# The recurrence's chunk matrices at 64 columns, all heads in one pass, products on 64x64 tiles of TensorE

## Chip, cores and metric

One core of one Trainium2 chip. The metric is the device time of one execution in microseconds (us), as the median of several runs; lower is better.

## What is computed

A network of three layers on 256 tokens of width 1024, all in f32. The first layer has latent attention beside a recurrence of the RWKV-7 kind and a mixture of 32 experts; two more layers with other mixers and dense feed-forward parts follow. The change lies in the recurrence of the first layer, 8 heads of 64 by 64:

```python
def step(state, inp):
    r_t, w_t, k_t, v_t, kk_t, a_t = inp
    sa = jnp.einsum('bhij,bhj->bhi', state, -kk_t)
    state = (state * w_t[:, :, None, :]
             + sa[..., :, None] * (kk_t * a_t)[..., None, :]
             + v_t[..., :, None] * k_t[..., None, :])
    return state, jnp.einsum('bhij,bhj->bhi', state, r_t)
```

Both kernels compute it in chunks of 64 tokens (CH), 4 chunks (NCH). In a chunk the steps become products of matrices, with a triangular 64 by 64 matrix for each head and chunk that has to be inverted.

## The kernel before

The program is a row of stages. In each, every engine has its own list of instructions, written out by hand, and the engines wait for each other by semaphores; at the end of a stage all engines meet at a barrier. Stages follow each other on TensorE (PE), VectorE (DVE), ScalarE (ACT), GpSimd (POOL) and SyncE (SP), which issues the loads. The recurrence stands at lines 955 to 1212 and runs twice, `for half in range(2)`, for four heads each time. All its operands are in SBUF already. Behind it, a stage (from line 1215) normalizes its output and loads w_o; later stages load the experts' weights.

One pass treats 8 systems (head of an even or odd column half `h2`, pair of heads `hp`, block of 128 tokens `a`). A system is a 128 by 128 matrix with two chunks on the diagonal; the blocks off the diagonal are zeroed by masks. Its six parts:

- start: products of beta and of kappa with alpha and rho (L1003; contraction over 64 rows, 128 weight columns, 256 moving columns), the transposed product (L1012); DVE multiplies each with a mask (L1161, L1162, L1168) and forms a first inverse of blocks of two (L1173 to L1176), in `inv` and transposed in `inv_t`;
- five levels, for blocks of 2, 4, 8, 16 and 32: GpSimd masks `low` for the level (L989), PE makes x = low_b times inv_t (L1023), ACT copies it to SBUF (L1125), PE multiplies with the inverse from both sides (L1032, L1036) and DVE adds the result to `inv_t` and `inv` (L1182, L1183). Each is done for two groups q of four systems, four matrices of 128 columns to a bank of 512. The last level has only the `inv_t` side;
- products with the inverse: a2v (L1042), za (L1050, L1052), ta (L1057), then the matrices that carry a chunk's state on, m (L1066) and n (L1075, L1076), these already as 64 by 64 products;
- the scan over four chunks, with the state of each (L1083, L1196 to L1203, ACT's copy L1144);
- u (L1093), added to za (L1207), and the output (L1102, L1110, L1111), copied to `hT` (L1147).

An f32 `matmul` of the code is two MATMUL records and two LDWEIGHTS records in the trace. Which rows of SBUF the operands lie in and which partitions of PSUM the result goes to sets the tile of the array that is used: "64*64" in a row of the trace is a tile of 64 rows and 64 columns, "128*128" the whole array. Four 64*64 tiles fit in it.

## Time and profile before

| | us |
|---|---|
| median of 3 runs | 2520.09 (2504.41 to 2524.5) |
| profiled execution, its own time | 2518.74 |
| span of its trace | 2517.0 |
| PE busy | 2293.7 |
| DVE busy | 1108.0 |
| ACT busy | 713.1 |
| POOL busy | 34.8 |
| both passes of the recurrence, 218.25 to 364.90 | 146.65 |

The span runs from the first to the last instruction, and times inside it are counted from its start. Busy time of PE includes modelled ends of pipelined matmuls, so neighbouring records overlap; the distance between starts says more. "PEclk" is the share of TensorE's 2.4 GHz that was granted: 1.00 is 2.4 GHz, 0.50 is 1.2 GHz.

### The profile page before, as it was taken

The page shows a single profiled execution, that of the slowest core. Times are in us where ns is not written, and L with a number is a line of the kernel's source. Part 1 is how long each engine was busy: PE and PEld are TensorE (multiplying, and loading weights), DVE is VectorE, ACT ScalarE, POOL GpSimd, SP SyncE. Part 2 cuts the span into 40 slices and gives each one's busy share as a digit, 9 for nine tenths or more (in the row PEclk, how much of TensorE's full clock was granted, in tenths as well). Part 3 has the DMA queues.
Part 4 walks back from the last instruction along what each step waited for, and adds up shares of the span by engine and source line. Part 5 has one row for each costly group of instructions (what it writes and reads, how often), then busy time and mean ns, then how long its engine had stood idle before and what let it go on. Part 6 is the DMA issues. An engine that isn't in the chain of part 4 may idle for free. (4 is left out here: it accounts for less than half of the span.)

```text
span 2517.0 us, 36320 instructions
## 1 busy us (share of the span) xinstructions
PE 2293.7 (91%) x14950; PEld 1670.3 (66%) x14950; DVE 1108.0 (44%) x1702; ACT 713.1 (28%) x912; POOL 34.8 (1%) x31
## 2 busy tenths in 40 slices
PE   6967787899999999999999799999999999999998
PEld 4635765443333333433333799988999999988998
DVE  4546434212111111211112655677755655677654
ACT  3332112101010000110101444544433433536332
POOL 0001110000000000000000000000000000000000
PEclk8967877899999999999999899999999999999999
DMA  9530015699999999999997555532655555423551
GB/s 392 222 153 1 1 67 216 280 424 425 426 426 425 425 426 425 425 425 426 425 413 283 177 175 183 168 118 84 201 185 183 179 186 182 156 94 120 189 183 67
DMA packets 236123, 626.84 MB, mean 249 GB/s; under 512 B 13144, under 2 KB 153976, under 8 KB 200056
## 3 DMA queue, kind: packets, MB, share of 16 engines
q1 hardware_dynamic: 232808, 622.35, 64.2%
q10 hardware_dynamic: 3216, 3.06, 0.4%
q8 instruction: 74, 1.21, 0.2%
q14 instruction: 25, 0.20, 0.0%
HBM read 624.33 MB, written 1.05 MB: 248 GB/s over the span
## 5 line engine op out<-in xcount | busy, mean ns | idle before, releaser
L1839 DVE TENSOR_TENSOR w_low<-ring,w_high 128x2048 fp32r<-128x2048 f32 x168 | 383.9, 2289 | 275.9 <-ACT w_high L1834 275.9
L1834 ACT ACTIVATE w_high<-ring 128x2048 fp32r<-128x2048 f32 x168 | 319.8, 1909 | 271.3 <-PE bank L2048 137.2
L1595 PE MATMUL bank<-ring,ut 128*64 128x512 f32 x1024 | 250.4, 641 | 48.3 <-DMA ring<-in_exp_w_dram 48.2
L1566 PE MATMUL bank<-ring,xt 128*64 128x512 f32 x1024 | 223.3, 594 | 0.3 <-ACT xt L1649 0.3
L1566 PE MATMUL bank<-ring_odd,xt 128*64 128x512 f32 x1024 | 223.3, 594 | 0.0
L1595 PEld LDWEIGHTS bank<-ring,ut 128*64 128x64 f32 x1024 | 73.9, 146 | 209.1 <-issue 127.5
L2063 PE MATMUL bank<-h_high,w_high 128*128 128x256 f32 x1408 | 187.4, 282 | 15.2 <-ACT h_high L1936 15.2
L2063 PEld LDWEIGHTS bank<-h_high,w_high 128*128 128x128 f32 x1408 | 176.0, 189 | 16.0 <-ACT h_high L1936 15.8
L2063 PE MATMUL bank<-h_high,w_low 128*128 128x256 f32 x1408 | 186.1, 281 | 0.0
L2063 PE MATMUL bank<-h_low,w_high 128*128 128x256 f32 x1408 | 186.0, 281 | 0.0
L2063 PEld LDWEIGHTS bank<-h_high,w_low 128*128 128x128 f32 x1408 | 175.7, 189 | 0.0
L2063 PEld LDWEIGHTS bank<-h_low,w_high 128*128 128x128 f32 x1408 | 175.4, 189 | 0.0
L1653 ACT ACTIVATE sg<-glu 128x512 f32<-128x512 f32 x32 | 20.2, 630 | 535.6 <-DVE glu L1716 535.6
L1566 PEld LDWEIGHTS bank<-ring,xt 128*64 128x64 f32 x1024 | 72.3, 137 | 143.2 <-issue 143.2
L1566 PEld LDWEIGHTS bank<-ring_odd,xt 128*64 128x64 f32 x1024 | 72.1, 137 | 142.9 <-issue 142.9
L1731 DVE TENSOR_TENSOR hT<-bank,hT 128x512 f32<-128x512 f32 x64 | 44.3, 691 | 249.8 <-PE bank L1609 249.7
L1715 DVE TENSOR_SCALAR lin<-bank 128x256 f32<-128x256 f32 x64 | 26.6, 416 | 256.1 <-PE bank L1566 256.1
L1708 DVE TENSOR_SCALAR choose<-base 128x128 fp32r<-128x128 f32 x32 | 9.1, 286 | 249.5 <-PE bank L1595 249.5
L1666 ACT ACTIVATE y<-bank 64x512 f32<-64x512 f32 x64 | 37.9, 592 | 273.4 <-PE bank L1595 272.6
L2048 PE MATMUL bank<-u_high,w_high 128*128 128x256 f32 x704 | 93.7, 283 | 4.9 <-DVE w_low L1839 4.9
L2048 PE MATMUL bank<-u_high,w_low 128*128 128x256 f32 x704 | 93.0, 281 | 0.0
L2048 PE MATMUL bank<-u_low,w_high 128*128 128x256 f32 x704 | 92.0, 279 | 0.0
(528 smaller groups left out, 3065.2 us busy)
## 6 DMA issues: line engine op xcount, KB each, us to landing
ring<-in_exp_w_dram SPq DMA_DIRECT2D x256, 1024.0 KB, 21.9
ring_odd<-in_exp_w_dram SPq DMA_DIRECT2D x128, 1024.0 KB, 21.0
ring<-in_ffn_w_gate_dram SPq DMA_DIRECT2D x44, 1024.0 KB, 5.3
ring<-in_ffn_w_up_dram SPq DMA_DIRECT2D x44, 1024.0 KB, 5.2
ring<-in_ffn_w_down_dram SPq DMA_DIRECT2D x44, 1024.0 KB, 4.8
ring<-in_w_in_dram SPq DMA_DIRECT2D x36, 1024.0 KB, 5.2
ring<-in_ada_w_dram SPq DMA_DIRECT2D x24, 1024.0 KB, 11.7
ring<-in_w_out_dram SPq DMA_DIRECT2D x8, 1024.0 KB, 5.2
```

Source lines behind the costliest of these rows:

```text
L1566: ins = nc.tensor.matmul(bank[b][at:at + SLOTS, :], xt[:, c, SLOTS * side:SLOTS * side + SLOTS], (ring, ring_odd)[side][:, c, 512 * q:512 ...
L1595: ins = nc.tensor.matmul(bank[2 + dh][64 * dh:64 * dh + 64, :], ut[:, r % 4, 64 * (r // 4):64 * (r // 4) + 64], w[:, x, 512 * dh:512 * dh ...
L1653: nc.scalar.activation(sg[:, :], glu[:, :], ACT.Sigmoid, scale=SW_ALPHA).then_inc(sem("sg_ready"), 1)
L1666: nc.scalar.activation(y[64 * side:64 * side + 64, 512 * dh:512 * dh + 512], bank[2 + dh][64 * dh:64 * dh + 64, :], ACT.Copy).then_inc(sem ...
L1708: nc.vector.tensor_scalar(choose[:, side, :], const("half_of"), const("expert_of")[:, bass.ds(e, 1)], None, ALU.mult).then_inc(sem("chosen ...
L1715: nc.vector.tensor_scalar(lin[:, 256 * b:256 * b + 256], pairs[:, :, 1], LIMIT, -LIMIT, ALU.min, ALU.max)
L1731: nc.vector.tensor_tensor(av, bank[6 + n % 2][:, :], av, ALU.add).then_inc(sem("acc_added"), 1)
L1834: nc.scalar.activation(w_bufs[0][u % BUFS], ring2[:, u % RING2, :], ACT.Copy).then_inc(high2, 1)
L1839: nc.vector.tensor_tensor(w_bufs[1][u % BUFS], ring2[:, u % RING2, :], w_bufs[0][u % BUFS].bitcast(F32), ALU.subtract).then_inc(low2, 1)
L2048: ins = nc.tensor.matmul(sums(m // 2)[:, T * (m % 2):T * (m % 2) + T], w[:, at:at + P], v[:, T * x:T * x + T], start=(g == 0 and k == 0 an ...
L2063: ins = nc.tensor.matmul(b[:, T * x:T * x + T], w[:, at:at + P], h[:, c, :], start=(k == 0 and x == 0 and c == 0), stop=(k == 2 and c == D ...
```

## The change

The recurrence becomes one stage for all 8 heads. It has 16 systems. A system's matrix is kept 64 columns wide: rows 0 to 63 hold the matrix of the first chunk of a block of 128 tokens, rows 64 to 127 that of the second, and the zero blocks are gone. Eight systems fill a bank of 512 columns, so an elementwise operation on 512 columns now covers eight systems instead of four, and the two groups q cover all 16. The constants are 64 columns wide too, with `above2` for both masks of a product at once; products of alpha and rho go through one operation of DVE.

Every product with such a matrix is now two, one for `ph` 0 in rows 0 to 63 and one for `ph` 1 in rows 64 to 127, each a 64 by 64 tile with 64 moving columns (128 in the beta and kappa products). In the levels, a2v and za the two write partitions 0 to 63 and 64 to 127 of the same bank; in the other parts the row tiles write different banks and four tiles take turns. The beta products come first, then the transposed product, then half of the kappa products; the other half stand behind the second level. ACT's first copy waits for its own half of the first inverse, and the two sides of a level have semaphores of their own (`growth_t`, `growth`, `inv_grown`). Buffers of the scan are twice as wide. The products of the scan stay 128 by 128, eight in the one scan where each of two scans had four.

The diff, cut to its core:

```diff
...
-    same = i[:, None] // CH == i[None] // CH
-    rwkv["above"] = same & (i[:, None] < i[None])
-    rwkv["below"] = same & (i[:, None] > i[None])
-    rwkv["above_eq"] = same & (i[:, None] <= i[None])
+    row, col = i[:, None] % CH, np.arange(CH)[None]
+    rwkv["above2"] = np.concatenate([row < col, row <= col], 1)
+    rwkv["below"] = row > col
+    rwkv["same"] = row == col
...
-        NS = 8
-        for half in range(2):
...
-                mats = [x.rearrange("p (s t) -> p s t", t=P) for x in ring_scratch]
-                lt, a3, a2, a4, low, inv_t, inv, low_b = mats
...
+        NS = HP * 2 * TT
+        with ExitStack() as c5, Stage(nc, pool) as S:
+            sem = S.sem
+            lt_a3, a2_a4 = (ring[:, SCRATCH + j, :].rearrange("p (s x t) -> p s x t", s=NS, x=2) for j in range(2))
+            lt, a3, a2, a4 = lt_a3[:, :, 0, :], lt_a3[:, :, 1, :], a2_a4[:, :, 0, :], a2_a4[:, :, 1, :]
+            low, inv, inv_t, low_b = (x.rearrange("p (s t) -> p s t", t=CH) for x in ring_scratch[4:8])
...
+            def system(h2, hp, a):
+                return 8 * h2 + 2 * hp + a
...
+            def half_rows(ph):
+                return slice(64 * ph, 64 * ph + 64)
...
+                def products(src, hq, bank_of):
+                    for hp in (2 * hq, 2 * hq + 1):
+                        for a in range(TT):
+                            at = 2 * P * (hp % 2) + P * a
+                            for h2 in range(2):
+                                for ph in range(2):
+                                    ins = nc.tensor.matmul(bank[bank_of(h2)][half_rows(ph), at:at + P], src[half_rows(h2), hp, tokens(a, ph)],
+                                                           alpha_rho[half_rows(h2), hp, :, tokens(a, ph)], start=True, stop=True)
+                    ins.then_inc(sem("products"), 1)
+                def grow(n, q):
+                    for s_ in range(8 * q, 8 * q + 8):
+                        for ph in range(2):
+                            r = half_rows(ph)
+                            ins = nc.tensor.matmul(bank[2 + q][r, CH * (s_ % 8):CH * (s_ % 8) + CH], inv[r, s_, :], xs[r, s_, :], start=True, stop=True)
+                    ins.then_inc(sem("growth_t"), 1)
+                    if n == len(LEVELS) - 1:
+                        return
+                    for s_ in range(8 * q, 8 * q + 8):
+                        for ph in range(2):
+                            r = half_rows(ph)
+                            ins = nc.tensor.matmul(bank[4 + q][r, CH * (s_ % 8):CH * (s_ % 8) + CH], xs[r, s_, :], inv[r, s_, :], start=True, stop=True)
+                    ins.then_inc(sem("growth"), 1)
+                for hq in range(2):
+                    products(beta, hq, lambda h2: 2 * hq + h2)
+                for hp in range(HP):
+                    for a in range(TT):
+                        at = CH * (2 * hp + a)
                         for h2 in range(2):
-                            for hp in range(2):
-                                for a in range(TT):
-                                    rows = slice(64 * h2, 64 * h2 + 64)
-                                    ins = nc.tensor.matmul(bank[b0 + 2 * h2 + hp][:, T * a:T * a + T], src[rows, 2 * half + hp, token(a)],
-                                                           alpha_rho[rows, 2 * half + hp, :, token(a)], start=True, stop=True)
-                                ins.then_inc(sem("products"), 1)
+                            for ph in range(2):
+                                ins = nc.tensor.matmul(bank[4 + h2][half_rows(ph), at:at + CH], alpha_rho[half_rows(h2), hp, 0, tokens(a, ph)],
+                                                       beta[half_rows(h2), hp, tokens(a, ph)], start=True, stop=True)
+                ins.then_inc(sem("low_product"), 1)
+                products(kappa, 0, lambda h2: 6 + h2)
+                for n, b in enumerate(LEVELS):
+                    for q in range(2):
+                        pe.wait_ge(sem("low_b_ready"), 2 * n + q + 1)
+                        pe.wait_ge(sem("inv_ready"), 2 * n + q + 1)
+                        if n == 0 and q == 0:
+                            pe.wait_ge(sem("products_taken"), 4)
+                            pe.wait_ge(sem("low_ready"), 2)
+                        for s_ in range(8 * q, 8 * q + 8):
+                            for ph in range(2):
+                                r = half_rows(ph)
+                                ins = nc.tensor.matmul(bank[q][r, CH * (s_ % 8):CH * (s_ % 8) + CH], low_b[r, s_, :], inv_t[r, s_, :],
+                                                       start=True, stop=True)
+                        ins.then_inc(sem("x_ready"), 1)
+                    for q in range(2):
+                        pe.wait_ge(sem("x_taken"), 2 * n + q + 1)
+                        if n:
+                            pe.wait_ge(sem("inv_grown"), 2 * (n - 1) + q + 1)
+                        grow(n, q)
+                    if n == KAPPA_LEVEL:
+                        pe.wait_ge(sem("products_taken"), 6)
+                        products(kappa, 1, lambda h2: 6 + h2)
...
+                def mask(dst, k, hq, b):
+                    dve.wait_ge(sem("products"), k)
+                    for h2 in range(2):
+                        s_ = system(h2, 2 * hq, 0)
+                        st.tell(nc.vector.tensor_tensor(dst[:, s_:s_ + 4, :, :].rearrange("p s x t -> p s (x t)"),
+                                                        bank[b + h2][:, :].rearrange("p (s x) -> p s x", s=4), above2, ALU.mult), "products_taken")
+                for hq in range(2):
+                    mask(lt_a3, hq + 1, hq, 2 * hq)
+                dve.wait_ge(sem("low_product"), 1)
+                for q in range(2):
+                    st.step(nc.vector.tensor_tensor(low[:, 8 * q:8 * q + 8, :], bank[4 + q][:, :].rearrange("p (s t) -> p s t", t=CH),
+                                                    eight("below"), ALU.mult), "low_ready")
+                for q in range(2):
+                    part = slice(8 * q, 8 * q + 8)
+                    st.step(nc.vector.tensor_tensor(inv[:, part, :], low[:, part, :], eight("lower1"), ALU.mult))
+                    st.step(nc.vector.tensor_tensor(inv[:, part, :], inv[:, part, :], eight("same"), ALU.add))
+                    st.step(nc.vector.tensor_tensor(inv_t[:, part, :], lt[:, part, :], eight("lower1_t"), ALU.mult))
+                    st.step(nc.vector.tensor_tensor(inv_t[:, part, :], inv_t[:, part, :], eight("same"), ALU.add), "inv_ready")
+                mask(a2_a4, 3, 0, 6)
...
```

How the order moves on PE, at the start of the recurrence. A row is one or more products with the same shape (x8 is eight of them; MATMUL here is one product, weight columns x moving columns), stageN are the semaphores waited for. Before, one pass:

```order
L1003 MATMUL bank<-alpha_rho,beta 128x256 x8
L1003 MATMUL bank<-alpha_rho,ps 128x256 x8
L1012 MATMUL bank<-beta,alpha_rho 128x128 [waits stage5]
L1012 MATMUL bank<-beta,alpha_rho 128x128 x3
L1012 MATMUL bank<-beta,alpha_rho 128x128 [waits stage5]
L1012 MATMUL bank<-beta,alpha_rho 128x128 x3
L1023 MATMUL bank<-ring 128x128 [waits stage1,stage7,stage2]
```

Now, for both halves of the heads (ps is kappa):

```order
L1012 MATMUL bank<-alpha_rho,beta 64x128 x32
L1037 MATMUL bank<-beta,alpha_rho 64x64 x32
L1012 MATMUL bank<-alpha_rho,ps 64x128 x16
L1052 MATMUL bank<-ring 64x64 [waits stage7,stage1,stage6,stage2]
L1052 MATMUL bank<-ring 64x64 x15
L1052 MATMUL bank<-ring 64x64 [waits stage6,stage2]
```

The transposed product no longer stands behind both kinds of products, and waits for no mask; 16 of the 32 kappa products have left the start.

One level on PE, before; stage2 is low_b_ready, stage7 inv_ready, stage8 x_taken:

```order
L1023 MATMUL bank<-ring 128x128 [waits stage7,stage2]
L1023 MATMUL bank<-ring 128x128 x3
L1023 MATMUL bank<-ring 128x128 [waits stage7,stage2]
L1023 MATMUL bank<-ring 128x128 x3
L1032 MATMUL bank<-ring 128x128 [waits stage8]
L1032 MATMUL bank<-ring 128x128 x3
L1036 MATMUL bank<-ring 128x128 x4
```

And now, where stage6 is inv_ready and stage11 inv_grown:

```order
L1052 MATMUL bank<-ring 64x64 [waits stage6,stage2]
L1052 MATMUL bank<-ring 64x64 x15
L1052 MATMUL bank<-ring 64x64 [waits stage6,stage2]
L1052 MATMUL bank<-ring 64x64 x15
L1020 MATMUL bank<-ring 64x64 [waits stage11,stage8]
L1020 MATMUL bank<-ring 64x64 x15
L1027 MATMUL bank<-ring 64x64 x16
```

The order inside a level is as it was; each group of four large products is a group of sixteen small ones, and there is one such level for all heads where there were two.

DVE at the start, before; L1161 and L1162 are the masks of one product, L1168 the mask `below`:

```order
L1161 TENSOR_TENSOR ring<-bank,rwkv_const 128x256 [waits stage4]
L1162 TENSOR_TENSOR ring<-bank,rwkv_const 128x256
...
L1168 TENSOR_TENSOR ring<-bank,rwkv_const 128x512 [waits stage6,stage5]
L1168 TENSOR_TENSOR ring<-bank,rwkv_const 128x512 [waits stage6,stage1]
L1161 TENSOR_TENSOR ring<-bank,rwkv_const 128x256 [waits stage4,stage1]
```

And now, where L1204 masks two kinds of product at once and L1211 is `below`:

```order
L1204 TENSOR_TENSOR ring<-bank,rwkv_const 128x512
L1211 TENSOR_TENSOR ring<-bank,rwkv_const 128x512 [waits stage5]
L1211 TENSOR_TENSOR ring<-bank,rwkv_const 128x512 [waits stage1]
L1215 TENSOR_TENSOR ring<-ring,rwkv_const 128x512 [waits stage1]
L1216 TENSOR_TENSOR ring<-ring,rwkv_const 128x512 [waits stage27]
L1217 TENSOR_TENSOR ring<-ring,rwkv_const 128x512 [waits stage27]
```

The kappa masks, eight operations between `below` and the first inverse before, now come behind the inverse.

## Rows read from the trace of the kernel before

**Rows 1.** The page: span, busy time and share of each engine.

```profile
span 2517.0 us, 36320 instructions
...
PE 2293.7 (91%) x14950; PEld 1670.3 (66%) x14950; DVE 1108.0 (44%) x1702; ACT 713.1 (28%) x912; POOL 34.8 (1%) x31
```

**Rows 2.** Windows over both passes: length, busy time by engine (instructions), clock, DMA.

```profile
core 0: us, PE busy (x) PEld busy (x) DVE busy (x) ACT busy (x) POOL busy (x), PEclk, DMA share, GB/s
218.25:230.50 12.25, 5.77 (x48) 5.34 (x49) 9.69 (x23) 0.00 (x0) 4.32 (x4) 0.89 0.00 0
230.50:240.10 9.60, 8.74 (x48) 8.48 (x49) 3.99 (x6) 1.19 (x2) 3.08 (x2) 0.61 0.01 2
240.10:263.30 23.20, 20.61 (x178) 19.96 (x178) 9.61 (x15) 4.78 (x8) 7.61 (x6) 1.00 0.00 1
263.30:275.00 11.70, 11.56 (x163) 11.18 (x161) 2.64 (x6) 3.10 (x11) 0.00 (x0) 1.00 0.01 1
275.00:279.40 4.40, 1.31 (x10) 1.07 (x10) 2.43 (x8) 1.85 (x6) 0.00 (x0) 0.95 0.01 2
279.40:289.80 10.40, 9.17 (x64) 8.18 (x65) 0.88 (x4) 0.77 (x2) 0.02 (x1) 0.69 0.01 2
289.80:302.00 12.20, 5.77 (x48) 5.32 (x48) 9.64 (x23) 0.00 (x0) 4.32 (x4) 0.90 0.00 0
302.00:312.00 10.00, 9.09 (x51) 8.85 (x52) 4.04 (x6) 1.20 (x2) 3.07 (x2) 0.62 0.01 2
312.00:334.80 22.80, 20.20 (x175) 19.56 (x174) 9.50 (x15) 4.78 (x8) 7.62 (x6) 1.00 0.00 1
334.80:346.60 11.80, 11.67 (x164) 11.29 (x162) 2.73 (x6) 3.10 (x11) 0.00 (x0) 1.00 0.01 1
346.60:351.90 5.30, 2.20 (x8) 1.85 (x9) 2.44 (x8) 1.85 (x6) 0.00 (x0) 0.56 0.00 0
351.90:364.90 13.00, 11.46 (x64) 10.16 (x64) 0.88 (x4) 0.77 (x2) 0.00 (x0) 0.50 0.00 1
sum 146.65, PE 117.55 PEld 111.24 DVE 58.50 ACT 23.39 POOL 30.03; mean PE 9.80 PEld 9.27 DVE 4.87 ACT 1.95 POOL 2.50
```

**Rows 3.** Timeline of SyncE behind the recurrence: start, us, what it issues.

```profile
364.90 5.29 SPq L275 DMA_DIRECT2D ring<-in_w_o_dram  x4
392.77 4.13 SPq L1336 DMA_DIRECT2D ring_odd<-in_exp_w_dram  x8
```

**Rows 4.** Windows: one level of the first pass.

```profile
241.84:248.09 6.25, 5.60 (x48) 5.44 (x49) 2.58 (x4) 1.19 (x2) 2.54 (x3) 1.00 0.00 0
```

**Rows 5.** Timeline, end of the start: start, us, instruction [idle before <- releaser].

```profile
229.71 0.69 DVE L1176 TENSOR_TENSOR ring<-ring,base 128x512 f32<-128x512 f32 x1
230.43 0.69 DVE L1173 TENSOR_TENSOR ring<-ring,rwkv_const 128x512 f32<-128x512 f32 x1
...
230.50 0.55 PE L1023 MATMUL bank<-ring 128*128 128x128 f32 x1 [6.46 <-DVE ring L1176]
```

**Rows 6.** Timeline of PE in a level.

```profile
244.60 1.06 PE L1032 MATMUL bank<-ring 128*128 128x128 f32 x8
245.49 1.06 PE L1036 MATMUL bank<-ring 128*128 128x128 f32 x8
246.38 1.06 PE L1023 MATMUL bank<-ring 128*128 128x128 f32 x8
```

**Rows 7.** Timeline of PE in n, and the line view of L1066.

```profile
272.20 0.33 PE L1075 MATMUL bank<-ring,nat 64*64 64x64 f32 x4
272.32 0.33 PE L1076 MATMUL bank<-nat 64*64 64x64 f32 x4
272.49 0.28 PE L1075 MATMUL bank<-ring,nat 64*64 64x64 f32 x2
272.60 0.28 PE L1076 MATMUL bank<-nat 64*64 64x64 f32 x2
```

```profile
L1066 PE MATMUL bank<-nat,ring x32: 218/218/267, 270.3 to 271.6; 64*64 64x64 f32 x32
```

**Rows 8.** Timeline of PE where the beta products end (ps is kappa).

```profile
220.40 0.38 PE L1003 MATMUL bank<-alpha_rho,beta 64*128 64x256 f32 x1
220.51 0.38 PE L1003 MATMUL bank<-alpha_rho,ps 64*128 64x256 f32 x1
220.62 0.38 PE L1003 MATMUL bank<-alpha_rho,beta 64*128 64x256 f32 x1
```

**Rows 9.** Timeline of the scan and the output, first pass.

```profile
275.75 0.29 DVE L1198 TENSOR_TENSOR plus<-state,step_n 128x128 f32<-128x128 f32 x1
...
279.38 2.03 PE L1093 MATMUL bank<-states,ta_t 128*64 128x128 f32 x16 [1.45 <-ACT states L1144]
...
281.33 1.78 PEld L1102 LDWEIGHTS bank<-alpha_rho,states 128*128 128x128 f32 x8 [0.33 <-issue]
```

**Rows 10.** Windows in the output stages of both passes.

```profile
282.40:285.80 3.40, 3.40 (x21) 3.20 (x20) 0.00 (x0) 0.00 (x0) 0.00 (x0) 0.50 0.00 0
285.80:289.20 3.40, 2.77 (x26) 2.31 (x24) 0.00 (x0) 0.77 (x2) 0.00 (x0) 1.00 0.00 0
354.00:357.40 3.40, 3.40 (x20) 3.28 (x21) 0.88 (x4) 0.00 (x0) 0.00 (x0) 0.50 0.00 0
357.40:360.80 3.40, 3.40 (x18) 2.95 (x15) 0.00 (x0) 0.39 (x1) 0.00 (x0) 0.50 0.00 0
```

More of the change, by code:

```diff
@@ L129, in shape_constants @@
     base["expert_of"] = (i[:, None] % 32 == np.arange(E)[None])
-    same = i[:, None] // CH == i[None] // CH
-    rwkv["above"] = same & (i[:, None] < i[None])
-    rwkv["below"] = same & (i[:, None] > i[None])
-    rwkv["above_eq"] = same & (i[:, None] <= i[None])
+    row, col = i[:, None] % CH, np.arange(CH)[None]
+    rwkv["above2"] = np.concatenate([row < col, row <= col], 1)
+    rwkv["below"] = row > col
+    rwkv["same"] = row == col
     for b in (1, 2, 4, 8, 16, 32):
-        m = (i[:, None] // (2 * b) == i[None] // (2 * b)) & (i[:, None] % (2 * b) >= b) & (i[None] % (2 * b) < b)
-        rwkv[f"lower{b}"] = m
-        if b == 1:
-            rwkv["lower1_t"] = m.T
+        rwkv[f"lower{b}"] = (row // (2 * b) == col // (2 * b)) & (row % (2 * b) >= b) & (col % (2 * b) < b)
+    rwkv["lower1_t"] = (row // 2 == col // 2) & (col % 2 >= 1) & (row % 2 < 1)
     rwkv["no_start"] = np.tile((np.arange(HP * T) % CH != 0), (P, 1))
@@ L1214, in build @@
+        if stop == "rwkv0":
+            return
         with ExitStack() as c6, Stage(nc, pool) as S:
```

425 lines of the change are left out of this document (196 added, 229 removed).

## The prediction

> **What bounds the kernel now.** I read the busy lines of the page first, then the span cut at the stages of the recurrence, then the timeline inside them. TensorE (PE) is busy for 91% of the span [rows 1], but that is a mean: what the change touches is the stretch from 218.25 to 364.90 us, 146.65 us long, and it is worth what that stretch loses. Nothing else runs beside it (DMA 0 to 2 GB/s in each of its windows), and SyncE issues the first load that the next stage needs, w_o, at 364.90 and the expert weights only at 392.77 [rows 2, 3]. So what the stretch loses comes off the whole span, one for one.
>
> The stretch is two passes with the same six stages: start (products, masks, first inverse) 12.25 and 12.20 us, level 0 9.60 and 10.00, levels 1 to 4 23.20 and 22.80, the products behind them 11.70 and 11.80, the scan over chunks 4.40 and 5.30, the output 10.40 and 13.00 [rows 2]. In levels 1 to 4 PE is the bound: busy 5.60 of the 6.25 us of a level, DVE 2.58, GpSimd 2.54, ACT 1.19 [rows 4]. In the start the masks are: DVE is busy 9.69 of 12.25 us and PE waits 6.46 us for it [rows 2, 5].
>
> **What a small product costs.** Each f32 product is two records in the trace. Four 128x128 ones with 128 columns are eight records, and each such group starts 0.89 us after the one before (244.60, 245.49, 246.38 [rows 6]): 0.111 us a record. The change makes of it two products of 64x64 with 64 columns, four records for two. What counts is the pitch of such a record, in us from start to start. The trace has three values. On one tile alone (rows L1075 and L1076 from 272.49 on, one pair each 0.117 us) it is 0.058. Where the program passes from one column tile to the other, eight records start between 272.20 and about 272.43: 0.029, both tiles at work at once [rows 7]. The mean over all 32 records of L1066, whose products pass from tile to tile after every eight records, is 1.3 us over 31 steps: 0.042 [rows 7]. Row tiles overlap too: beta and kappa products of L1003, which the program has one after the other, alternate between 220.40 and 220.94, each kind 0.21 us after its last and one record every 0.11 us [rows 8]. The new code changes tile after every product, two records, so its pitch should lie between 0.029 and 0.058. I take 0.0425, the measured mean of the nearest row, since nothing shows 0.029 kept up for hundreds of records. At 0.0425 two small products cost 4 x 0.0425 = 0.17 us against 0.223 for the large one: PE gains a quarter, DVE, ACT and GpSimd a half, as every one of their operations now carries 512 useful columns.
>
> **The sum, stage by stage, after against before (both passes).**
>
> Start and level 0, before 12.25 + 9.60 + 12.20 + 10.00 = 44.05 us. After: 32 records of 128 columns at 0.054 (two tiles at once, each at 0.11) bring the first mask to 2.1 us. The order puts 64 such records and 64 of 64 columns ahead of the `below` mask: 3.5 + 2.7, with 0.3 for the semaphore 6.5 us, by which the four masks (0.69 each [rows 5]) are done. Then two `below` masks to 7.95 and eight operations on the inverses of 0.725 to 13.8 us. x of the first half of the systems and its copy lie in this wait; the two kappa masks come behind it on DVE and lie beside PE. From 13.8 on level 0 has 160 records: 6.8 us. The clock was at 0.61 in this stage [rows 2], with PE just off its wait; I keep it at 1.2 GHz until 20.4 us, which costs 3.3 us. Together 23.9, saving 20.2.
>
> Levels 1 to 4, before 46.00. After 3 x 192 + 128 = 704 records, 29.9 us, and 32 records of 128 columns (kappa, behind level 1) 1.7: 31.6, saving 14.4. No wait is left on PE here. The longest ring of one level is x of half the systems (32 records, 1.4), 0.3 to ACT, copy 0.6, growth 1.4, 0.3 to DVE, addition 0.7, 4.7 us in all, against 192 x 0.0425 = 8.2 us of PE work. DVE's 2.8 us, ACT's 1.2 and GpSimd's 2.5 in a level [rows 4], now once for both passes, stay under it.
>
> Products behind the levels, before 23.50. After 64 (a2v) + 128 (za) + 64 (ta) + 64 (m) + 128 (n) = 448 records, 19.0 us, saving 4.5. The four copies of za, 0.69 each, lie beside za and ta.
>
> Scan, before 9.70. After: one scan with operations twice as wide. Two copies of step_n 1.5, seven operations of 0.46 (0.29 for 128 columns [rows 9], some 0.17 more for 256) 3.2, two rounds of eight records at 0.111 with 0.3 behind each 2.4, last copies 0.5: 7.6, saving 2.1.
>
> Output, before 23.40. After: 32 records for u at 0.12, the price at 1.2 GHz (16 in 1.95 us [rows 9]), 3.9; 32 with the states at 0.22 (8 in 1.78), 7.1; 128 small ones 5.4; copies and barrier 1.9. Together 18.3, saving 5.1. If the clock doesn't come back for the 128, 5.4 more.
>
> Sum after 23.9 + 31.6 + 19.0 + 7.6 + 18.3 = 100.4 us, against 146.65: 46.3 us saved. The profiled execution took 2518.74 us (span 2517.0), 1.35 below the median of 2520.09; 2518.7 - 46.3 = 2472.4, and I forecast 2472, 1.8 or 1.9% less. The cleared buffers double to some 1.9 us each on GpSimd, hidden since they are needed past 30 us; the smaller table of constants is loaded a stage earlier.
>
> The whole result hangs on the pitch: behind the start there are 160 + 704 + 448 + 128 = 1440 small records, so each ns of pitch is 1.44 us. At 0.029 everywhere the gain is 46.3 + 19.4, and with the start 2 us shorter and the clock never low in level 0 some 71 us: 2448, my lower end. At 0.0425 + 46.3/1440 = 0.075 nothing is gained.
>
> **Rivals.** First: tiles don't overlap, pitch 0.058 at 2.4 GHz. For it: in the levels both tiles write one bank, rows 0 to 63 and 64 to 127, whereas the overlapping row tiles of [rows 8] write different banks, so this very case is not in the trace. Against it: L1066's column tiles share one bank and overlap, only their row tile is common. Price 15.5 x 1.44 = 22.3, and 0.053 more on each of the 96 records of 128 columns, 5.1: 2518.7 - 18.9 = 2500.
> The Trainium skill, "TensorEngine Tiling (Array Packing)", section "Restrictions and Gotchas", says that "Different row tiles cannot access same PSUM bank simultaneously", with no word on different partitions of it; by that rule this rival is the result.
> The Trainium skill, "TensorE: Matmul & The Clock Gate", section "Wait — 56ns, not 53.3ns?", gives 62 ns per matmul where its instructions are decoded in software, which would give about the same time; the 42 ns of L1066 speaks against it, but only over 32 records that may have been decoded ahead.
>
> Second: tiles overlap well, but the clock stays at 1.2 GHz through the levels. For it: the same instructions get either level. From 282.4 to 285.8 PE is busy throughout at 0.50 and is granted 1.00 right after; in the second pass they keep it busy from 354 to 360.8 and it stays at 0.50 [rows 10]. And the new start has the same waits of PE after which it was low before. Against it: the 64x64 products of both passes ran at 1.00 [rows 2]. Price: pitch 0.058 from overlapping at half speed, 22.3, and 1.7 for kappa: 2495.
>
> Third, the other side: clock low and one tile at a time, pitch 0.116. Price 73.5 x 1.44 = 106, 3.3 of it already counted, 8.5 more for the records of 128 columns: 111 - 46 = 65 us slower, 2584. It decides from a pitch of 0.075 on, and is slower by over 1% from 0.093.
>
> Fourth: the gain is given back later. The rest of the chain is serial through two more layers and the expert weights are requested after the recurrence, so little speaks for it; a shifted clock in later stages may cost 5 to 10 us. If all: 2519.
>
> **How the numbers follow.** Forecast case (pitch up to 0.05, mostly full clock) 0.62, first rival 0.12, second 0.17, third 0.06, fourth 0.03. A measurement here tells about 1%, 25 us, from no change. Faster by over 1% (below 2495) is the forecast case and half of the first two, with a little taken off: 0.75. Slower is the third and a rest of the fourth: 0.07. Within 1% is the rest, 0.18. The range runs from 2448 to 2506, past the first two rivals; only the third and its neighbours lie outside above.
>
> **What would show it.** The stretch from the first product to w_o's load near 100 us. Small records starting every 0.03 to 0.05 us, pairs at rows 0 and 64 together. In levels 1 to 3 PE busy without a gap, about 8 us a level, at 1.00; x of the second half starting 13.8 us in. A level of over 14 us, or PE clock 0.50 through the levels, would prove me wrong; PE idle in the levels would mean that some copy or mask, not PE, is the bound.

## The result, and the profile after

The changed kernel took 2431.62 us (median of 4 runs, 2429.74 to 2432.24), the kernel before 2515.2 (4 runs, the first three among them, 2504.41 to 2524.5): a ratio of 0.9672, 95% interval 0.9634 to 0.9709. The forecast was 2472 with a range from 2448 to 2506. The direction was right; the gain is some 83 us and not 46, and the time lies below the range. A second timing, told of below, gave 0.9715 (0.9671 to 0.9758), some 70 us.

The profiled execution took 2429.74 us. Its page, against [rows 1]:

```profile
span 2427.6 us, 37626 instructions
...
PE 2207.3 (91%) x15686; PEld 1601.2 (66%) x15686; DVE 1086.4 (45%) x1638; ACT 703.2 (29%) x883; POOL 21.8 (1%) x19
```

The windows of the recurrence, columns as in [rows 2]: start, level 0, levels 1 to 4, the products behind them, and scan with output.

```profile
208.15:218.03 9.88, 3.79 (x160) 3.59 (x161) 8.49 (x11) 0.00 (x0) 6.96 (x4) 0.94 0.01 2
218.03:229.02 10.99, 8.95 (x192) 8.79 (x194) 7.08 (x9) 1.19 (x2) 2.54 (x2) 0.59 0.01 3
229.02:250.43 21.41, 21.41 (x744) 21.41 (x740) 10.98 (x17) 4.78 (x8) 7.49 (x6) 1.00 0.02 4
250.43:260.30 9.87, 9.16 (x404) 8.89 (x400) 3.50 (x6) 3.75 (x9) 0.00 (x0) 1.00 0.02 5
260.30:283.00 22.70, 14.62 (x259) 13.78 (x259) 6.56 (x14) 4.21 (x11) 0.00 (x0) 0.77 0.01 2
sum 74.85, PE 57.92 PEld 56.47 DVE 36.62 ACT 13.93 POOL 16.99; mean PE 11.59 PEld 11.29 DVE 7.32 ACT 2.79 POOL 3.40
```

The stage takes 74.85 us where both passes took 146.65. In levels 1 to 4 PE is busy for every one of 21.41 us at full clock. SyncE's two loads behind the recurrence, against [rows 3]:

```profile
282.96 5.16 SPq L273 DMA_DIRECT2D ring<-in_w_o_dram  x4
309.24 4.25 SPq L1382 DMA_DIRECT2D ring_odd<-in_exp_w_dram  x8
```

The spans differ by 2517.0 - 2427.6 = 89.4 us, and the landmarks divide it. Ahead of the recurrence 218.25 - 208.15 = 10.1; the recurrence 71.8; from w_o's load to the expert weights' (27.87 to 26.28) 1.6; from there to the first expert load behind the router, at 459.93 and 370.88, 67.16 to 61.64, 5.5; the rest 0.3. The two stretches behind the recurrence run the same code as before; what differs there is the clock, 0.58 and 0.80 before (columns as in [rows 2]):

```profile
364.90:392.77 27.87, 14.12 (x28) 8.14 (x29) 14.78 (x18) 4.46 (x6) 0.00 (x0) 0.58 0.58 185
392.77:459.93 67.16, 50.11 (x218) 39.77 (x218) 24.87 (x76) 20.22 (x33) 1.80 (x1) 0.80 0.46 188
```

and 0.74 and 0.86 after:

```profile
282.96:309.24 26.28, 11.97 (x35) 8.03 (x36) 14.79 (x18) 4.24 (x6) 0.00 (x0) 0.74 0.61 196
309.24:370.88 61.64, 44.60 (x210) 35.23 (x211) 24.88 (x75) 20.32 (x34) 1.80 (x1) 0.86 0.50 205
```

PE is busy 50.11 us of the second stretch before and 44.60 after, 5.5 less, which is all that the stretch is shorter; DVE's and ACT's busy times are the same to 0.1 us.

What fills the 74.85 us can be read in four places of the timeline. First, PE in one level, against [rows 4] and [rows 6] (L1052 is x, L1020 and L1027 the growth from both sides):

```profile
241.10 2.04 PE L1052 MATMUL bank<-ring 64*64 64x64 f32 x64
242.96 1.11 PE L1020 MATMUL bank<-ring 64*64 64x64 f32 x32
243.90 1.11 PE L1027 MATMUL bank<-ring 64*64 64x64 f32 x32
244.83 1.11 PE L1020 MATMUL bank<-ring 64*64 64x64 f32 x32
245.76 1.11 PE L1027 MATMUL bank<-ring 64*64 64x64 f32 x32
246.70 0.51 PE L1052 MATMUL bank<-ring 64*64 64x64 f32 x11
```

Groups of 32 records start 0.93 us apart: a pitch of 0.029 us, both tiles at work all the time, though they write one bank. A level is 5.60 us for all heads.

Second, the start, DVE and GpSimd with PE's first x, against [rows 5] (L1204 masks two kinds of product, L1211 is `below`, L1215 to L1218 form the first inverse, L1000 is GpSimd's mask of a level):

```profile
211.73 1.41 DVE L1211 TENSOR_TENSOR ring<-bank,rwkv_const 128x512 f32<-128x512 f32 x2
213.18 0.69 DVE L1215 TENSOR_TENSOR ring<-ring,rwkv_const 128x512 f32<-128x512 f32 x1
213.22 3.44 POOL L1000 TENSOR_TENSOR ring<-ring,rwkv_const 128x512 f32<-128x512 f32 x2 [1.54 <-DVE ring L1211]
213.90 1.64 DVE L1216 TENSOR_TENSOR ring<-ring,rwkv_const 128x512 f32<-128x512 f32 x1
...
215.57 1.63 DVE L1217 TENSOR_TENSOR ring<-ring,rwkv_const 128x512 f32<-128x512 f32 x1
217.24 0.69 DVE L1218 TENSOR_TENSOR ring<-ring,rwkv_const 128x512 f32<-128x512 f32 x1
...
218.03 1.97 PE L1052 MATMUL bank<-ring 64*64 64x64 f32 x32 [6.08 <-DVE ring L1218]
```

Operations of DVE that take 0.69 us take 1.64 while GpSimd works on SBUF too.

Third, PE in m and n, where four tiles take turns (against [rows 7]):

```profile
257.66 0.97 PE L1103 MATMUL bank<-nat,ring 64*64 64x64 f32 x50 [0.16 <-issue]
...
258.59 0.27 PE L1117 MATMUL bank<-nat 64*64 64x64 f32 x4
...
261.40 0.27 PE L1117 MATMUL bank<-nat 64*64 64x64 f32 x2 [1.65 <-issue]
```

50 records start within 0.76 us (257.66 to 258.42): 0.015 each, all four tiles at work. Then PE sits idle for 1.65 us in the middle of n with nothing to wait for but its own instructions.

Fourth, scan and output, against [rows 9]:

```profile
262.46 1.42 DVE L1235 COPY step_n<-bank 128x512 f32<-128x512 f32 x2 [5.47 <-PE bank L1117]
...
264.49 1.79 PE L1124 MATMUL bank<-state,step_m 128*128 128x64 f32 x8 [2.06 <-DVE state L1241]
267.33 1.97 PE L1124 MATMUL bank<-state,step_m 128*128 128x64 f32 x8 [1.05 <-DVE state L1247]
271.58 4.09 PE L1133 MATMUL bank<-states,ta_t 128*64 128x128 f32 x32 [2.28 <-ACT states L1190]
275.60 3.79 PE L1142 MATMUL bank<-alpha_rho,states 128*128 128x64 f32 x32
...
279.31 0.34 PE L1151 MATMUL bank<-ring,w_kv 64*64 64x64 f32 x8
```

### The profile page after: what moved, and what is told of

The parts are those of the page before. It is cut to its first block and busy times, and to the rows that moved or that the text cites. A ratio compares the mean times of both kernels' runs of the same rounds, so it can differ in the third digit from the quotient of the medians.

```text
span 2427.6 us, 37626 instructions
## 1 busy us (share of the span) xinstructions
PE 2207.3 (91%) x15686; PEld 1601.2 (66%) x15686; DVE 1086.4 (45%) x1638; ACT 703.2 (29%) x883; POOL 21.8 (1%) x19
```

## The experiments

In all of them the recurrence is measured from its first memset to w_o's load: 146.67 us before, 74.84 after. The single time of before beside the first eight is 2510.62 us.

**What is chance: both kernels once more.** `before_again` and `after_again` are unchanged.

> The kernel before, unchanged, profiled once more. Of the 89.4 us between the two spans, 17.6 lie outside the recurrence: 10.1 ahead of it and 7.5 behind it, in code that the change leaves alone. Theory: there the clock was granted differently by chance, so this trace shows other lengths ahead of the recurrence (its start anywhere from 208 to 218 us) with the recurrence itself again at 146 +-4 us. Rival: the changed kernel shortens them by itself; then this trace repeats 218 us for the start and 95 us from the end of the recurrence to the first expert load after the router.

2518.29 us. The recurrence begins at 215.13 (218.23 in the first trace), takes 146.59, and the two stretches behind it 27.90 and 67.10.

> The changed kernel, unchanged, profiled once more, as the measure for the other three. The stage of the recurrence 74.8 +-1 us; its start anywhere from 208 to 220 us, since that stretch varied by as much in kernels with the same code there; from w_o's load to the first expert load behind the router 88 us again, against 95 in both traces of the kernel before.

2447.57 us, 16 more than the first runs of the same kernel. The recurrence begins at 220.02, twelve us later than in the first trace, takes 75.91, and 87.7 us follow for the two stretches behind it; from the end of these to the end of the program it takes 5.2 us more than in the first trace. So the stretch ahead varies from run to run, and its clock with it (from 130 us on, 0.74 in the first trace of the change and 0.62 here), in kernels that are the same there; over the twelve traces of kernels with narrow matrices the recurrence began between 205.0 and 220.0. The 10.1 us ahead lie inside that scatter: they are chance. The gain right behind the recurrence is not: the two stretches together take 95.0 us in both traces of before and 87.6 to 90.5 in the twelve of kernels with narrow matrices, the router's stretch 67.1 against 61.6 to 63.6.

**Does it hang on the order of the tiles?** `tile_order` issues all products of one tile before those of the other, in the levels alone:

```diff
-                    for s_ in range(8 * q, 8 * q + 8):
-                        for ph in range(2):
+                    for ph in range(2):
+                        for s_ in range(8 * q, 8 * q + 8):
```

> The changed kernel with the loops over systems and over ph swapped in x and in both growths: sixteen records on one tile, then sixteen on the other, the same products. Theory (the gain of PE is that two tiles work at once, which needs neighbours in the order to lie on different tiles): the mean pitch rises from 0.029 to between 0.042 and 0.055 us, a level from 5.6 to 8 to 10.5 us, the recurrence 14 to 22 us longer than its 74.8. Rival (PE reorders as far as it likes, or the pitch is set by the supply of instructions and not by the tiles): a level stays at 5.6 us and the time within 3 us.

2466.09 us; the recurrence takes 100.32, 25.5 more than after and above both theories. PE in levels, at half clock (first row) and at full clock (the others), and windows of levels 0 and 1 and of a later level:

```profile
240.90 2.61 PE L1027 MATMUL bank<-ring 64*64 64x64 f32 x26
...
264.52 1.50 PE L1020 MATMUL bank<-ring 64*64 64x64 f32 x26
...
266.03 1.50 PE L1027 MATMUL bank<-ring 64*64 64x64 f32 x26
```

```profile
229.00:243.50 14.50, 14.50 (x173) 14.50 (x174) 4.05 (x6) 1.19 (x2) 2.54 (x2) 0.50 0.01 2
243.50:261.70 18.20, 18.20 (x235) 18.20 (x232) 3.46 (x5) 1.19 (x2) 2.53 (x2) 0.50 0.01 2
...
270.33:279.38 9.05, 9.05 (x196) 9.05 (x196) 2.77 (x4) 1.20 (x2) 2.53 (x2) 1.00 0.01 2
```

At full clock a level is 9.05 us, against 5.60: 32 records in 1.51 us, 0.047 each. Most of them start 0.058 us after the last, as on one tile; only at a switch of tiles do three pairs start within 0.006 us of each other. With level 0's 160 records the levels have 864, and 864 x 0.018 = 15.6 us of the 25.5. The other 10 go with the clock, by what is left over. It stays at 0.50 over all of the 32.7 us of the first two windows, with PE busy throughout; after has it low for 10.2 us, nearly all in level 0. The lost overlap is the order's doing. Whether the low clock would come with this order each time, one run can't say; in the nine other traces with one pass and tiles in turn it was low there for 13.7 us at most.

**Does one pass matter, beside the narrow products?** `narrow_two_passes` has the narrow matrices and alternating tiles, but two passes of four heads:

```diff
-        NS = HP * 2 * TT
-        with ExitStack() as c5, Stage(nc, pool) as S:
+        NS = 8
+        for half in range(2):
+            with ExitStack() as c5, Stage(nc, pool) as S:
...
-                        for s_ in range(8 * q, 8 * q + 8):
+                        for s_ in range(4 * q, 4 * q + 4):
```

> 64 columns and 64x64 tiles as in the change, but again two passes of four heads, so elementwise operations of 256 columns in the levels and twice the start, scan and barrier. Theory (the tiles and the dropped zero blocks bring most, the merged pass saves repeated waits only): the recurrence takes 85 to 97 us, against 146.65 before and 74.8 changed. Rival (the merged pass brings most, since each pass is bound by its waits): over 110 us.

2452.97 us; the recurrence takes 88.83, 14.0 more than after and 57.8 less than before. One level of one pass:

```profile
224.90:227.94 3.04, 3.02 (x103) 2.89 (x101) 1.71 (x5) 0.77 (x2) 1.41 (x2) 1.00 0.00 0
```

Two such levels are 6.08 us, one of after 5.60. So four fifths of what the recurrence gained are the narrow products, and one fifth is the single pass. A timed pair followed, both kernels in the same rounds:

> The changed kernel again, timed against the one before in rounds. By its traces 71 to 72 us come from the recurrence and 7 from the better clock behind it: 78 to 80 us or a ratio of 0.968 to 0.970; the 2431.6 of the first measurement had a few us of luck ahead of the recurrence, so a median of 2430 to 2447.

> narrow_two_passes, timed. Its trace had 88.8 us in the recurrence, 14 more than the changed kernel, and 90.5 behind it against 88: 12 to 18 us more than after_timed.

The change took 2441.65 us (2431.26 to 2444.13), the two passes 2459.06 (2445.3 to 2465.22), before 2511.23 (7 runs, 2500.51 to 2518.03): ratios of 0.9715 (0.9671 to 0.9758) and 0.9806 (0.9761 to 0.9851). The second pass costs 17.4 us by the medians; the two ranges lie only 1.2 us apart. In their traces the recurrence takes 76.05 and 89.12, 13.1 apart: from the start to the first x 9.9 against twice 6.0, from there to a2v 32.8 against twice 18.3, and from u to the end 11.6 against twice 8.9 (its first pass doubled). Each half-size pass pays its waits, its first and last copies and its barrier again; the levels themselves give 3.8 of the 13.1.

**What stops PE inside n?** `n_twice` computes n a second time into the same banks, 128 records more.

```diff
+                for hp in range(HP):
+                    for a in range(TT):
...
+                                nc.tensor.matmul(bank[ph][half_rows(h2), at:at + 64], nat[r, 1, a, head_cols(h2, hp)],
+                                                 za[r, system(h2, hp, a), 64:P], start=True, stop=False)
```

> The changed kernel with the products of n (L1112, L1117: 128 records on four tiles, 0.0146 us apart while they run) done twice, with the same result. Theory (256 instructions, LDWEIGHTS and MATMUL of 128 records, are one 16 KB load of the instruction queue, and a next one is there no sooner than 3.7 us after the last was entered): n takes 3.7 us more. Rival (the gap of 1.87 us inside n is a single event): 1.9 us more, with one gap as before.

2445.58 us; the recurrence takes 78.99. From the first product of m to the scan it takes 11.28 us, where after, `after_again` and `after_timed` have 7.44, 7.51 and 7.77: 3.5 to 3.8 more. Two idle times stand in n now, each behind 128 records:

```profile
273.43 0.27 PE L1117 MATMUL bank<-nat 64*64 64x64 f32 x2 [1.36 <-issue]
...
277.44 0.27 PE L1130 MATMUL bank<-nat 64*64 64x64 f32 x2 [1.91 <-issue]
```

From 269.98 over 273.43 to 277.44 each round of 128 records took 3.45 and 4.0 us, though their starts take under 2. `n_two_tiles` orders n so that only two tiles take turns:

```diff
-                for hp in range(HP):
-                    for a in range(TT):
-                        at = 64 * (HP * a + hp)
-                        for h2 in range(2):
+                for h2 in range(2):
+                    for hp in range(HP):
+                        for a in range(TT):
+                            at = 64 * (HP * a + hp)
```

> The changed kernel with n in another order: the column tile changes only half way, so two tiles work at once where four did, 128 records 0.029 us apart instead of 0.0146. Theory (the supply of instructions, 128 records in 3.7 us, bounds n already): the recurrence stays within 0.5 us of 74.8, and the gap inside n is gone. Rival (four tiles at once are worth their pitch): 1.9 us longer.

2438.68 us, recurrence 75.24. Four records now take 0.117 us, half the pace, and the idle time shrinks from 1.65 to 0.44 us:

```profile
265.54 0.28 PE L1112 MATMUL bank<-ring,nat 64*64 64x64 f32 x4
265.66 0.28 PE L1116 MATMUL bank<-nat 64*64 64x64 f32 x4
...
267.78 0.27 PE L1116 MATMUL bank<-nat 64*64 64x64 f32 x2 [0.44 <-issue]
```

From m to the scan it takes 7.68 us, inside the 7.44 to 7.77 of the three traces of the change. Four tiles at work are no faster here than two.

Does the same limit stand behind the levels' 0.029? `half_width` keeps every instruction of the levels and gives each product 32 weight and 32 moving columns:

```diff
-... bank[2 + q][r, CH * (s_ % 8):CH * (s_ % 8) + CH], inv[r, s_, :], xs[r, s_, :], ...
+... bank[2 + q][64 * ph:64 * ph + 32, CH * (s_ % 8):CH * (s_ % 8) + 32], inv[r, s_, 0:32], xs[r, s_, 0:32], ...
```

> The changed kernel with the products of the levels (x and both growths) cut to 32 weight columns and 32 moving columns each, as many instructions as before; three quarters of each result are left out, so the numbers are not the reference's. Theory (in the levels the 0.029 us pitch is the array's, two tiles at 0.058 each, and the supply of instructions is only just not the bound): with half the columns the array needs 0.015, but 128 records still take 3.7 us, so a level stays at 5.5 us or more. Rival (instructions come faster than that when PE takes them steadily): a level falls to 3 to 4 us and the recurrence to about 65 us.

2428.45 us; the recurrence takes 73.71, and levels 1 to 4 take 20.0 us (228.71 to 248.72) against 21.41. Half the columns saved a fifteenth, though one level, at 4.74 us, was shorter than the 5.5 expected. PE in the levels:

```profile
239.22 0.41 PE L1020 MATMUL bank<-ring 64*32 64x32 f32 x14 [1.22 <-issue]
...
239.95 1.32 PE L1052 MATMUL bank<-ring 64*32 64x32 f32 x64
...
242.93 0.41 PE L1020 MATMUL bank<-ring 64*32 64x32 f32 x14 [1.13 <-issue]
...
246.45 0.95 PE L1052 MATMUL bank<-ring 64*32 64x32 f32 x48 [1.31 <-issue]
```

The 64 records of x start within 1.13 us, 0.018 each, and then PE is idle: it resumes at 239.22, 242.93 and 246.45, 3.7 and 3.5 us apart, with 127 records in the trace between each. The DMA view of the same 12 us (236 to 248) shows what comes at this pace:

```profile
DMA packets 4, 0.07 MB, mean 5 GB/s; under 512 B 0, under 2 KB 0, under 8 KB 0
...
q8 instruction: 4, 0.07, 2.4%
```

Four packets of 16 KB on the instruction queue and nothing else. Each starts 3.6 to 3.7 us after the last, and 128 MATMUL with their 128 LDWEIGHTS records (127 in the trace) lie between two waits. So where PE waits for instructions it gets 128 small records per 3.5 to 4.0 us, 0.027 to 0.031 each; the shortest distance of two packets in the recurrence of any trace is 3.35 us, in `two_passes_timed`. Two tiles on 64 columns use them at 0.029, 128 in 3.7 us. So I take the levels of after to stand at both limits at once; in `after_again` one level took 5.94 us instead of 5.60, with a wait of 0.12 us at "issue" in it.

**What does the low clock cost?** After has 10.2 us of half clock in level 0 and 10.3 in scan and output. `warm_start` fills PE's wait ahead of level 0 with five products of 512 columns that nothing reads; `warm_all` adds nine of 256 columns in the waits of the scan:

```diff
+                def fill(n, b, columns):
+                    for _ in range(n):
+                        nc.tensor.matmul(bank[b][:, 0:columns], ident, nat[:, 3, 0, 0:columns], start=True, stop=True)
...
+                pe.wait_ge(sem("products_taken"), 4)
+                fill(5, 2, 512)
```

> The changed kernel with five f32 products of 128x128 with 512 columns more, into a bank that is free, in PE's wait for the first inverse; nothing reads their result. Theory (level 0 runs at 1.2 GHz because PE stood idle for 6 us before it): the clock is at 1.00 in level 0, whose 160 records behind the second x take 4.7 us instead of about 7, the recurrence 2 to 4 us shorter. Rival (the 64x64 products themselves bring the clock down or don't keep it up): level 0 has half the clock again and the time stays or grows by up to 2 us.

2441.69 us, recurrence 73.39, between 1.4 and 2.7 less than in the three traces of the change (74.84, 75.91, 76.05), where 2 to 4 were expected. Level 0 takes 10.15 us against 10.99, 11.31 and 11.37. The windows show the clock at 1.00 through the start and low for 3.4 us only:

```profile
218.10:228.00 9.90, 8.27 (x170) 5.40 (x171) 8.48 (x11) 0.00 (x0) 6.99 (x4) 1.00 0.01 2
228.00:231.90 3.90, 1.15 (x32) 1.03 (x32) 3.76 (x5) 0.60 (x1) 1.26 (x1) 1.00 0.00 0
231.90:235.30 3.40, 3.37 (x63) 3.40 (x65) 1.21 (x2) 0.60 (x1) 1.27 (x1) 0.50 0.02 5
```

> As warm_start, and nine products of 128x128 with 256 columns more in PE's waits of the scan, into a bank that is free. Theory: the clock, at 0.5 for 10 us from the scan to the middle of the output, stays at 1.00; the two state products take 0.9 us instead of 1.8 and u 2 us instead of 4, so 3 to 5 us less than warm_start. Rival: the added products delay those of the scan by as much as they gain, within 1 us of warm_start.

2440.38 us, recurrence 73.18. The clock was low for 3.4 us in scan and output instead of 10, and from u to the output's last part it took 6.2 us instead of 7.5. But the scan began at 57.5 us into the stage instead of 55.0. Of these 2.4 us 1.9 had passed when n was done, ahead of the first product that `warm_all` adds: up to there both kernels have the same instructions, yet PE waited 2.8 us at "issue" in `warm_all`, in three places, and 1.4 us in one place in `warm_start`, as the last packets of instructions came some 4.0 us apart and not 3.4 to 3.5. The added products themselves delayed the scan by 0.5 us, and from its first product to the end the stage took 15.7 us instead of 18.4. So what the clock gave was taken mostly by a slower supply of instructions that this change didn't cause; one trace of each can't say what `warm_all` is worth.

`warm_and_masks` goes further: eight filling products, two of them in the wait between the two x of level 0, and the two kappa masks of DVE, which read PSUM, ahead of the first inverse, so that they and not the inverse run beside GpSimd.

```diff
+                mask(a2_a4, 3, 0, 6)
                 for q in range(2):
                     part = slice(8 * q, 8 * q + 8)
...
-                mask(a2_a4, 3, 0, 6)
```

> warm_start with six products instead of five in the first wait and two in the second, and DVE's two kappa masks ahead of the first inverse, while GpSimd masks the first level. Theory (DVE's operations from SBUF to SBUF took 1.6 us instead of 0.7 where they met GpSimd's, those that read PSUM don't; PE stays warm): x of level 0 starts no later than the 9.9 us of the changed kernel although 1.3 us of masks stand ahead, no half clock in level 0, recurrence 72 to 73.5 us. Rival (masks meet GpSimd's operations as well): x starts at 11 us or later and the recurrence is again 74 us or longer. In the whole, against the changed kernel, 1 to 3 us less, which is hardly beyond its scatter.

2431.61 us (4 runs, 2428.22 to 2439.09), 0.9694 of before (0.9651 to 0.9736); the recurrence takes 74.38 against 76.05 in `after_timed`. Its start, its level 0 and its levels 1 to 4:

```profile
210.40:220.60 10.20, 9.14 (x173) 5.81 (x174) 8.76 (x13) 0.00 (x0) 6.51 (x4) 1.00 0.01 2
220.60:229.20 8.60, 7.74 (x197) 6.40 (x198) 5.68 (x7) 1.20 (x2) 2.54 (x2) 1.00 0.01 2
229.20:251.70 22.50, 22.05 (x743) 21.70 (x739) 11.02 (x17) 4.78 (x8) 7.49 (x6) 1.00 0.02 4
```

The clock is 1.00 throughout, and level 0 takes 8.60 instead of 10.99. The masks gained nothing that shows: the first x comes at 10.2 us, where after has 9.9. Levels 1 to 4 then take 22.50 instead of 21.41, with waits at "issue" before x (PE 0.36 us at 236.35, its weight loads 0.22 at 247.81). The median lies 10 us under `after_timed`, but the ranges overlap, the first runs of the change had 2431.62 too, and the stage accounts for 1.7 of it. A version faster than the change is not shown.

## Why the prediction was wrong in size

By its own steps, forecast against measured (the stage begins at 208.15):

| | forecast | measured |
|---|---|---|
| start and level 0 | 23.9 | 20.9 |
| levels 1 to 4 | 31.6 | 21.4 |
| products behind them, to 262.3 | 19.0 | 11.9 |
| scan, to 271.58 | 7.6 | 9.3 |
| output | 18.3 | 11.4 |
| sum | 100.4 | 74.9 |

**The step that failed** is a term of the sum, the price of a small record: "I take 0.0425, the measured mean of the nearest row, since nothing shows 0.029 kept up for hundreds of records." It was kept up for all 704 records of the levels, and where four tiles take turns the records came at 0.015. The levels alone hold 704 x (0.0425 - 0.029) = 9.5 of the 10.2 us that they came out shorter; the products hold 7.1, and the output's 128 small records, 2.0 us instead of 5.4, 3.4. The nearest row was the wrong kind of row. L1066 passes to the other tile after eight records, the new code after two. `tile_order`, which passes after sixteen, has 0.047, most records 0.058 apart: such a figure is a mean of stretches on one tile, and not of what two tiles do together. At each of the three switches inside L1066 the trace of before has three pairs of records that start within 0.006 us of each other; there the true pace could be read.

**The second mis-sized term** is the output's product with the states, priced 32 x 0.22 = 7.1. The 0.22 was of products with 128 moving columns [rows 9]; the new ones have 64 ("128x64"), and 32 took 3.7 us.

**The start** came out where forecast by two errors that cancel. The second x stood at 13.9 us (forecast 13.8). But `below` was done at 5.0 us and not 7.95, since all four tiles share the first products, 64 of 128 columns in 1.77 us; and the eight operations on the inverse took 8.7 us and not 5.8, since three of them ran beside GpSimd at 1.6 to 1.8 us. The change brought that about: before, the kappa masks stood between `below` and the inverse, and they read PSUM. `warm_and_masks` put two of them back there, where they took 0.69 and 0.68 us beside GpSimd; two operations of the inverse still met GpSimd's masks at 1.64 and 1.66 us, and the start didn't get shorter.

**Level 0** was at half clock as foreseen; its 160 records took 7.0 us, 0.044 each, where the forecast had 6.8 + 3.3. **The scan** was 1.7 longer: its two rounds of products fell into a stretch at half clock and took 1.8 and 2.0 us, where 0.9 and 0.3 behind it were priced.

**The cause behind the recurrence was not forecast at all.** I put in "a shifted clock in later stages may cost 5 to 10 us" as a loss; it gave 7. That it comes with the narrow matrices is shown by fourteen traces, two of before and twelve with them. That it is the clock is read from the windows above, where the same code has a higher clock and less busy time of PE and of no other engine; no run changed the clock alone. Why PE's clock is better there, no run tells.

**The range.** Its lower end, 2448, stood for 71 us saved, all of them in the recurrence, with 0.029 everywhere and no low clock in level 0. The recurrence saved 71.8. That these agree is in part luck: that figure left out what shortened the stage further (0.015 in the four-tile parts, the output's halved columns) and what made it longer (half clock in level 0, a slower scan, PE's wait for instructions in n). What put the time below the range lies outside the stage: the 7 us behind it, and in the first timing the 10 us of chance ahead. The step that failed there is the fourth rival's term, which counted a shifted clock as a loss only. 2518.7 - 71.8 - 7.1 is 2439.8, and the second timing has 2441.65.

**The rivals.** The first, one tile at a time because both write one bank, is refuted by the level's rows: 0.029 with both tiles in one bank, rows 0 to 63 and 64 to 127. The Trainium skill, "TensorEngine Tiling (Array Packing)", section "Restrictions and Gotchas", says that "Different row tiles cannot access same PSUM bank simultaneously"; the trace doesn't agree for tiles on different partitions. The Trainium skill, "PSUM — Partial Sum Buffer", section "PSUM bank collisions raise a hardware error", speaks of a bank within a partition quadrant, and with that the trace agrees. The other ground named for this rival, a price of some 0.06 us a record whatever the tiles, is refuted by the same rows and by 0.015 where four tiles take turns. The second (which by its own terms comes to 2496 and not 2495), half clock through the levels, came true for 10 us in level 0 (13.7 in two more traces of the same kernel), and for over 30 in `tile_order`: it was a real risk. The third, both at once, is nearest to what `tile_order` had for its first two levels (173 records in 14.50 us, 0.084 each, and not 0.116), and even so that run was 44 us faster than before. The fourth had the wrong sign.

**What stays open.** Why the clock stayed low so long in `tile_order` and came back so soon in the change; how much of the 7 us behind would be kept after another change; how far the levels would get faster with less time per record, since `half_width` got no more than a fifteenth; and what makes `after_again` 5.2 us longer behind the router.

## What to carry to other kernels

When a product is cut into tiles, price it by rows in which the tiles change as often as in the new code, and look for the pace over the few records around a switch of tiles, not for a line's mean. Issue neighbouring products to different tiles in turn: the same instructions in blocks of sixteen took 9.05 us a level instead of 5.60. Count the instructions too: below about 0.03 us a product record (128 records in 3.5 to 4.0 us), PE waited for its instructions here, and narrower or better packed products gained next to nothing.

## What the runs showed that I had not expected

- **Instructions are a resource.** 128 product records with their weight loads are one packet of 16 KB on the instruction queue. Where PE waited for them, a packet came every 3.6 to 3.7 us (`half_width`), 3.45 to 4.0 by the waits in `n_twice`; the shortest distance was 3.35 (`two_passes_timed`). The Trainium skill, "Runtime: NRT & Kernel Launch", section "Instruction fetch mechanics", has blocks of 16 KiB or 256 instructions, with a cost of crossing that is "mostly hidden"; the size agrees with the trace, the second doesn't where tiles are small: with four of them on 64 columns PE was idle for 1.65 of 3.74 us (257.66 to 261.40).
- **A slow stretch may fill the store.** After half clock in level 0 the levels ran without a gap in two of the three traces of the change, and `warm_start`, with 3.4 us of it, had none either; without any (`warm_and_masks`) they had gaps and took 1.1 us more. That the slow stretch lets instructions gather, so that part of what a better clock gives is taken back, is a reading and not shown: the packets came anywhere from 3.4 to 4.2 us apart, even where two kernels had the same instructions (`warm_start`, `warm_all`).
- **DVE and GpSimd on SBUF.** A DVE operation with two inputs in SBUF took 1.64 us instead of 0.69 beside GpSimd's mask, and GpSimd's two took 3.44 instead of the 2.50 that they have in the levels. DVE's masks that read PSUM weren't slowed.
- **The order of the tiles and the clock.** With the same products in another order the clock was at 0.50 for 32.7 us of levels with PE busy, against 10.2 us; that is one run.
